# Second attention of an encoder kernel: stationary values for both heads, and inverse sums spread over partitions through memory

## The chip, the cores and the metric

One core of one Trainium2 chip runs the kernel. The metric is the device time of one execution in microseconds (us), given as the median of several runs. The engines are PE (TensorE), DVE (VectorE), ACT (ScalarE), POOL (GpSimd) and SP (SyncE, which only issues transfers). Each works through its own list of instructions in order and is held up only by waits on semaphores. PE adds its products into PSUM, eight banks of 128 x 512 floats.

## What is computed

A trunk of two layers over 512 tokens of 1,024 features. Each layer is a token mixer and then an MLP with squared ReLU and 4,096 hidden features, an RMS norm stands before each, and one more at the end. Layer 0 mixes by neighbourhood attention, layer 1 by the sliding-window attention that the change is about. The reference, cut to that part:

```python
def sliding_window_gqa(h, w_qkv, sinks, rel_table, w_o):   # 16 heads of 64, 4 key/value heads
    ...
    kb, vb = band(k), band(v)                              # 3 key blocks of 128 per query block
    s = jnp.einsum('bnqhgd,bnjhd->bhgnqj', q, kb)          # logits, per block of 128 queries
    s = jnp.where(mask, s + bias, lowest)
    m = jnp.maximum(jnp.max(s, axis=-1, keepdims=True), sink)
    p = jnp.exp(s - m)
    p = p / (jnp.sum(p, axis=-1, keepdims=True) + jnp.exp(sink - m))
    o = jnp.einsum('bhgnqj,bnjhd->bnqhgd', p, vb).reshape(B, S, D)
    return jnp.einsum('bsd,de->bse', o, w_o)
```

## The kernel before

**Data.** Activations lie by feature (128 features on the partitions, 512 tokens along the row). Each float32 operand of a product is split into a high part (what fp32r holds) and a low part, the rest; a product is three matmuls: high x high, high x low, low x high (lines 427 to 429). Weights come as 180 chunks of 512 KB through two buffers: SP loads chunk c (L292) once chunk c-2 has been split, ACT copies out the high part (L839), DVE subtracts for the low part (L1140).

**The second attention.** It works by pairs of heads, 8 pairs, the two heads on key/value heads that lie beside each other in one 128-row tile. A pair has 4 units (n = 0 to 3), one per block of 128 queries, with 2, 3, 3 and 2 key blocks. For a unit:
- PE: scores of both heads (`sw_scores`, L729/L730) into `s_ps`.
- DVE: adds the bias and takes the row's extreme (`sw_logits`, L1232), one instruction per head.
- ACT: exponent and row sum, one per head (`sw_exp`, L918).
- PE: transposes the probabilities, one 128 x 128 block per head and key block (`sw_transpose`, L741), into `pt_ps`.
- ACT copies out the high part (`sw_pt_high`, L923), DVE the low part (`sw_pt_low`, L1189).
- PE: `sw_values` (L752 on, matmuls at L561 and L565): the transposed probabilities are the stationary operand, a head's values the moving one (64 columns of high, 64 of low). Output: 128 tokens on the partitions.

Two units make a group (g = 0, 1). After its second unit DVE (`sw_o_sum`) forms 1/(row sum + sink), adds the two halves of the output (reduce, L1197) and multiplies by the inverse (L1199): tokens lie on partitions, so the inverse is one number per partition. PE transposes that result back to features (`transpose_o`, L574), ACT and DVE split it (`sw_o_high` L1069, `sw_o_low` L1453) for the output projection.

**Order.** It is written out by hand in a `sw_step(m)` for each engine; step m handles pair p = m-1 and interleaves the dense projections of later pairs. PE, for each n: transposes of the unit before, [`transpose_o` at n = 0 and 2], one dense part (3 matmuls of 512 columns), scores of the next unit, a second dense part, values of the unit before. `pt_ps` and `s_ps` hold one unit each. After step 8 the output projection starts: 32 early blocks in the order of `EARLY_BLOCKS`, the last four of which (from the 28th) need the last pair's output.

SP has no order of its own here: it loads chunks in a loop. POOL loads each pair's bias with 8 transfers (L369), two pairs ahead.

```python
for n in range(4):                                  # PE, step m
    if before or n >= 1:
        sw_transpose(*sw_unit_by(p, n, -1))
    ...
    dense_part(2 * n)
    if n < 3 or last != 8:
        sw_scores(*sw_unit_by(p, n, 1))
    dense_part(2 * n + 1)
    if before or n >= 1:
        sw_values(*sw_unit_by(p, n, -1))
```

Of the kernel before, what the change touches and what calls it, by code (L numbers as in the profile page):

```python
# [100 lines left out]
def encoder(nc, xT, wstream, gains, rpb, sinks, rel_table, na_mask, onehot, out):  # L101
    t5_dram = nc.dram_tensor("t5_shifted", (QC, HEADS, T5_W), F32, kind="Internal").ap()
    rpb_dram = nc.dram_tensor("rpb_reversed", (HEADS, RPB_R * PITCH), F32, kind="Internal").ap()

    with ExitStack() as ctx:
# [80 lines left out]
        o_added, o_summed, ot_done, esink_made = sem("o_added"), sem("o_summed"), sem("ot_done"), sem("esink_made")  # L186
# [16 lines left out]
        def f32(ap):  # L203
            return ap.bitcast(F32)
# [67 lines left out]

        def sw_unit_by(p, n, by):

            return p + (n + by) // 4, (n + by) % 4
# [12 lines left out]
        def _(sp):  # L288
# [4 lines left out]

            load_weights(At(0))
# [13 lines left out]
            with sp.Fori((CH_SW + len(SW_FIRST)) // 2, CHUNKS // 2) as i:  # L308
                for n in range(2):
                    load_weights(At(n, 2, i))  # L310
# [113 lines left out]
        def _(pe):  # L424
# [131 lines left out]
            def values(dst, tiles, v_blocks, hh):  # L556

                last = len(tiles) - 1
                for b, (t, n) in enumerate(zip(tiles, v_blocks)):
                    def low():  # L560
                        nc.tensor.matmul(dst[:, HD * hh:HD * (hh + 1)], pt_lo[:, t, :], v_hi[:, n, hh, :], start=False,  # L561
                                         stop=False)
                    if b:
                        low()
                    ins = nc.tensor.matmul(dst, pt_hi[:, t, :], v_parts[:, n, hh, :, :].rearrange("p a b -> p (a b)"),  # L565
                                           start=b == 0, stop=b == last)
                    if not b:
                        low()
                return ins

            def transpose_o(done, bank):
                pe.wait_ge(o_summed, (done + 1).v)
                for jj in range(2):
                    ins = nc.tensor.transpose(bank[:, jj, :], o_tok[:, jj, :, :].rearrange("p a b -> p (a b)"), ident[:])  # L574
                ins.then_inc(ot_done, 1)

# [53 lines left out]
            def output_projection(ch, gr, heads_before, start, bank):  # L630

                early_part(ch, gr, heads_before, start, LAST_OUT)
                if bank is not None:
                    transpose_o(At(heads_before + HEADS - 1), bank)
                else:
# [98 lines left out]
            def sw_transpose(p, n):  # L734
# [3 lines left out]
                at = 0  # L738
                for hh in range(2):
                    for b in range(SW_BLOCKS[n][1]):  # L740
                        ins = nc.tensor.transpose(pt_ps[:, at, :], sw_probs(n, hh)[:, b * P:(b + 1) * P], ident[:])  # L741
                        at += 1
                ins.then_inc(pt_done, 1)

            def sw_values(p, n):

                kb, nb = SW_BLOCKS[n]
                pe.wait_ge(pt_split, (sw_unit(p, n) + 1).v)
                if n % 2 == 0:
                    pe.wait_ge(o_split, (p * 2 + (HEADS - 1 + n // 2)).v)  # L750
                for hh in range(2):
                    ins = values(sw_bank(n // 2)[:, 2 * hh + n % 2, :], range(nb * hh, nb * hh + nb),  # L752
                                 range(4 * p.odd + kb, 4 * p.odd + kb + nb), hh)
                ins.then_inc(pv_done, 1)
# [7 lines left out]
            def sw_step(m, before=True, last=None):  # L762
# [905 lines left out]
```

## Time and profile before

| | |
|---|---|
| device time, median of 3 runs (lowest to highest) | 1143.95 us (1143.48 to 1144.02) |
| time of the profiled execution | 1143.62 us |
| its span in the trace | 1141.9 us |
| TensorE's clock granted over the span | 0.998 of full speed |
| PE, DVE, ACT busy share of the span | 99%, 56%, 45% |
| second attention with its projections | 623.6 to 760 us of the span |
| a step of it (steps 2 to 7) | 15.28 to 15.31 us |

The span is what the trace covers; the 1.7 us between span and time lie around it. Steps were found by the first transposes of a pair's last unit, at 637.63, 652.93, 668.21, 683.49, 698.78, 714.09 and 729.38 us.

### The profile page before, as it was taken

Reading aid. Unit: us, or ns where it says so; the run is one execution under the profiler, and the core shown is the slowest. Engines: PE = TensorE matmul, PEld = TensorE weight load, DVE = VectorE, ACT = ScalarE, POOL = GpSimd, SP = SyncE. Lnnn points to the kernel's source line nnn. Section 1 sums busy time; section 2 is a strip of 40 time slices with the busy share of each in tenths; the row PEclk is TensorE's granted clock in tenths of the full one; section 3 lists DMA queues with packets and bytes.
Section 4 is the critical chain, followed back from the end, with each engine's and each line's share of the span. In section 5 each row is a group of like instructions: output and inputs, shape, how many; then the busy total and the mean of one; then the engine's idle time right before and its main releaser. Section 6 shows DMA issues by size and latency. Waiting matters only on the chain.

```text
span 1141.9 us, 16574 instructions
## 1 busy us (share of the span) xinstructions
PE 1130.5 (99%) x5580; PEld 943.7 (83%) x5580; DVE 638.3 (56%) x1030; ACT 513.1 (45%) x922; POOL 141.5 (12%) x243
## 2 busy tenths in 40 slices
PE   8999999999999999999999999999999999999997
PEld 6888888888888888888888888988888888888886
DVE  7788887764442234544346888866443223444334
ACT  6777677553331124433235676644443122333221
POOL 6544341330000000000001222100000000000000
PEclk9999999999999999999999999999999999999999
DMA  6332221333322332222322122122222222232222
GB/s 227 95 89 92 91 91 55 92 120 102 100 92 92 100 102 92 92 98 86 110 92 92 43 59 62 52 92 93 92 92 98 105 92 92 96 106 92 92 92 93
DMA packets 34290, 106.97 MB, mean 94 GB/s; under 512 B 5760, under 2 KB 8096, under 8 KB 34256
## 3 DMA queue, kind: packets, MB, share of 16 engines
q1 hardware_dynamic: 29344, 98.61, 25.8%
q0 software_dynamic: 4768, 7.90, 3.0%
q8 instruction: 20, 0.33, 0.1%
q14 instruction: 14, 0.11, 0.0%
q10 hardware_dynamic: 144, 0.02, 0.0%
HBM read 103.84 MB, written 2.67 MB: 93 GB/s over the span
## 4 chain that ended last, share of the span: by engine, by line
PE 98%; DVE 1%; ACT 0%; issue 0%; DMA 0%; DVEq 0%; ACTq 0%
PE acc L427 28%; PE acc L428 28%; PE acc L429 28%; PE om_ps L565 2%; PE pt_ps L741 2%; PE om_ps L589 1%; PE om_ps L561 1%; PE s_ps L531 1%; PE pt_ps L552 1%; PE s_ps L730 1%; PE s_ps L729 1%; PE om_ps L521 1%; PE s_ps L427 1%; PE s_ps L428 1%; PE s_ps L429 1%; DVE sqsum L1262 0%
## 5 line engine op out<-in xcount | busy, mean ns | idle before, releaser
L839 ACT CAST w_hi<-w_raw 128x1024 fp32r<-128x1024 f32 x179 | 188.3, 1052 | 391.9 <-PE acc L429 386.9
L427 PE MATMUL acc<-h_hi,w_hi 128*128 128x512 f32 x792 | 315.6, 398 | 1.0 <-DVE h_lo L1252 0.5
L429 PE MATMUL acc<-h_hi,w_lo 128*128 128x512 f32 x792 | 308.8, 390 | 0.0
L428 PE MATMUL acc<-h_lo,w_hi 128*128 128x512 f32 x792 | 308.8, 390 | 0.0
L1140 DVE TENSOR_TENSOR w_lo<-w_raw,w_hi 128x1024 fp32r<-128x1024 f32 x177 | 217.7, 1230 | 141.4 <-ACT w_hi L839 140.8
L427 PE MATMUL acc<-u_hi,w_hi 128*128 128x512 f32 (+1 forms) x624 | 240.7, 386 | 0.0
L429 PE MATMUL acc<-u_hi,w_lo 128*128 128x512 f32 (+1 forms) x624 | 239.5, 384 | 0.0
L428 PE MATMUL acc<-u_lo,w_hi 128*128 128x512 f32 (+1 forms) x624 | 239.4, 384 | 0.0
L427 PEld LDWEIGHTS acc<-h_hi,w_hi 128*128 128x128 f32 x792 | 148.7, 188 | 32.9 <-issue 1.7
L429 PEld LDWEIGHTS acc<-h_hi,w_lo 128*128 128x128 f32 x792 | 148.7, 188 | 31.7
L428 PEld LDWEIGHTS acc<-h_lo,w_hi 128*128 128x128 f32 x792 | 148.9, 188 | 28.4 <-issue 0.7
L1169 DVE SCALAR_TENSOR_TENSOR scaled<-acc,rstd 128x512 f32<-128x512 f32 x90 | 61.9, 689 | 138.8 <-PE acc L429 137.2
L427 PEld LDWEIGHTS acc<-u_hi,w_hi 128*128 128x128 f32 x624 | 117.3, 188 | 23.3 <-DVE w_lo L1140 0.5
L429 PEld LDWEIGHTS acc<-u_hi,w_lo 128*128 128x128 f32 x624 | 117.2, 188 | 23.1
L428 PEld LDWEIGHTS acc<-u_lo,w_hi 128*128 128x128 f32 x624 | 117.3, 188 | 22.5
L1314 DVE TENSOR_TENSOR x_res<-acc,x_res 128x512 f32 (+1 forms) x39 | 26.9, 691 | 99.5 <-PE acc L429 99.5
L918 ACT ACTIVATE probs<-probs,nmax 128x256 f32<-128x256 f32 (+1 forms) x128 | 67.4, 531 | 9.5 <-DVE nmax L1232 9.3
L352 POOL TENSOR_TENSOR bias_masked<-bias_pairs,mask 128x256 f32<-128x256 f32 x64 | 52.6, 859 | 83.3 <-DVE nmax L1232 81.4
L1179 DVE TENSOR_TENSOR u_lo<-scaled,u_hi 128x512 f32 (+1 forms) x72 | 53.6, 744 | 13.1 <-ACT u_hi L893 13.1
L923 ACT CAST pt_parts<-pt_ps 128x1024 fp32r<-128x1024 f32 (+2 forms) x48 | 38.5, 802 | 45.5 <-PE pt_ps L741 38.1
L1189 DVE TENSOR_TENSOR pt_parts<-pt_ps,pt_parts 128x1024 fp32r<-128x1024 f32 (+2 forms) x48 | 46.0, 957 | 14.6 <-ACT pt_parts L923 14.2
L410 POOL CAST u_hi<-u_hi 64x512 fp32r<-64x512 f32 x4 | 3.4, 858 | 365.5 <-DVE u_hi L1479 365.3
(158 smaller groups left out, 1076.3 us busy)
## 6 DMA issues: line engine op xcount, KB each, us to landing
w_raw<-in_wstream SPq DMA_DIRECT2D x180, 512.0 KB, 3.3
bias_pairs<-rpb_reversed POOLq DMA_DIRECT2D x64, 62.0 KB, 2.4
bias_pairs<-t_shifted POOLq DMA_DIRECT2D x64, 48.0 KB, 2.5
x_res<-in_xT SPq DMA_DIRECT2D x8, 256.0 KB, 5.5
out_y<-x_res SPq DMA_DIRECT2D x8, 128.0 KB, 1.8
out_y<-x_res SPq DMA_DIRECT2D x4, 256.0 KB, 2.3
t_shifted<-vT POOLq DMA_DIRECT2D x16, 31.0 KB, 2.1
mask<-in_mask POOLq DMA_DIRECT2D x1, 64.0 KB, 5.3
```

The lines of the kernel that those rows point to most:

```text
L352: ins = nc.gpsimd.tensor_tensor(bias_m[:, g, i, :, :].rearrange("p c r -> p r c"), rows[:, :, U0[j]:U0[j] + WC], mask[:, j:j + 1, :].to_br ...
L427: nc.tensor.matmul(dst, a[0], b[0], start=start, stop=False)
L428: nc.tensor.matmul(dst, a[0], b[1], start=False, stop=False)
L429: return nc.tensor.matmul(dst, a[1], b[0], start=False, stop=stop)
L839: nc.scalar.copy(w_hi[:, c.odd, :], w_raw[:, c.odd, :]).then_inc(w_hi_made, 1)
L918: return nc.scalar.activation(src, src, ACT.Exp, bias=nmax[:, slot, i:i + 1], scale=-1.0, accum_out=rsum[:, slot, i:i + 1])
L923: nc.scalar.copy(pt_hi[:, 0:blocks, :], pt_ps[:, 0:blocks, :]).then_inc(pt_hi_made, 1)
L1140: nc.vector.tensor_tensor(w_lo[:, c.odd, :], w_raw[:, c.odd, :], f32(w_hi[:, c.odd, :]), ALU.subtract).then_inc(w_split, 1)
L1169: nc.vector.scalar_tensor_tensor(out=dst, in0=order(bank), scalar=factor, in1=order(rstd[:]), op0=op, op1=ALU.mult).then_inc(acc_taken, 1)
L1179: nc.vector.tensor_tensor(order[0](dst), order[1](scaled[:, e.odd, :]), order[0](f32(hi)), ALU.subtract).then_inc(tile_split, 1)
L1189: nc.vector.tensor_tensor(pt_lo[:, 0:blocks, :], pt_ps[:, 0:blocks, :], f32(pt_hi[:, 0:blocks, :]), ALU.subtract).then_inc(pt_split, 1)
L1314: nc.vector.tensor_tensor(x[:, k.v, :], acc[g.odd][:], x[:, k.v, :], ALU.add).then_inc(acc_taken, 1)
```

## The change

For the second attention alone:
- **Values.** A stationary operand now is one key block's values of both heads side by side (128 columns: head 0, head 1), high or low. The moving operand is the transposed probabilities of both heads and of one or both units of the group: 256 or 512 columns. A group takes 9 matmuls: two key blocks that both units need (3 each, 512 columns) and one that only one unit needs (3 of 256 columns). Of the output, the rows of a head are used only in that head's columns. It lies by feature, so `transpose_o` and the reduce are dropped.
- **Place.** The values of group 0 run at the end of n = 2, those of group 1 at the end of n = 0 of the next step; none run at n = 1 and n = 3.
- **Inverse sums.** They must now lie along the row, the same on all 64 partitions of a head. SP stores the 128 x 4 inverses transposed to memory (4-byte runs), waits for that, and loads them back twice, each time 1 KB to 64 partitions. These steps (`turn_inverse`) stand in SP's list before and after the loads of weights, which are written out for the 8 steps.
- **Normalisation.** `sw_normalise` multiplies PSUM by the spread inverses, one instruction per head, at the head of DVE's n = 0 (group 0) and after the logits of n = 2 (group 1). The probabilities lie in a free part of `u_lo`, the values' parts in another order, the spread inverses in `vT`.
- **ACT.** `sw_o_high` now reads SBUF; it and `queries_high` stand ahead of the exponents, and the sinks of group 1 behind the split of weights.

The diff, cut to its core:

```diff
@@ SP
+            def turn_inverse(p, g):
+                sp.wait_ge(den_made, (p * 4 + (HEADS + 2 * g + 2)).v)
+                if p.a >= 1:
+                    sp.wait_ge(o_summed, (p * 2 + (HEADS - 1 + g)).v)
+                sp.dma_start(rden_dram[g].rearrange("t q -> q t"), dens_of(rden, g), allow_slow_non_contiguous=True).then_inc(rden_stored, 16)
+                sp.wait_ge(rden_stored, (p * 32 + 16 * (g + 1)).v)
+                for hh in range(2):
+                    sp.dma_start(sw_rden[HEAD_ROWS[hh], g, :], rden_dram[g, 2 * hh:2 * hh + 2, :].rearrange("t q -> (t q)").partition_broadcast(HD)
+                                 ).then_inc(rden_landed, 16)
+            def sw_step(m, before=True):
+                if before:
+                    turn_inverse(m + -2, 1)
+                load_weights(m + (CH_SW + 7))
+                turn_inverse(m + -1, 0)
...
+            for m in range(1, PAIRS + 1):
+                sw_step(At(m), before=m > 1)
+            turn_inverse(At(7), 1)
@@ PE
-            def sw_values(p, n):
...
+            def sw_values(p, g):
+                pe.wait_ge(pt_split, (sw_unit(p, 2 * g + 1) + 1).v)
+                pe.wait_ge(o_summed, (p * 2 + (HEADS - 1 + g)).v)
+                dst = flat(sw_bank(g)).rearrange("p (h u q) -> p h u q", h=2, u=2)
+                def products(b, units, start=False, stop=False):
+                    block = 4 * p.odd + g + b
+                    stationary = [t[:, block, :, :].rearrange("p h d -> p (h d)") for t in (sw_v_hi, sw_v_lo)]
+                    for n, (v, t) in enumerate(((0, 0), (0, 1), (1, 0))):
+                        ins = nc.tensor.matmul(dst[:, :, units, :], stationary[v], sw_pt[:, t, b, :, units, :],
+                                               start=start and n == 0, stop=stop and n == 2)
+                    return ins
+                both, only = ((0, 1), 2) if g == 0 else ((1, 2), 0)
+                products(both[0], slice(0, 2), start=True)
+                products(only, slice(1 - g, 2 - g))
+                products(both[1], slice(0, 2), stop=True).then_inc(pv_done, 2)
@@ PE, sw_step
-                    if n == 0 and before:
-                        transpose_o(p * 2 + (HEADS - 2), sw_bank(0))
-                    if n == 2 and before:
-                        transpose_o(p * 2 + (HEADS - 1), sw_bank(1))
...
-                    if before or n >= 1:
-                        sw_values(*sw_unit_by(p, n, -1))
+                    if n == 0 and before:
+                        sw_values(p + -1, 1)
+                    if n == 2:
+                        sw_values(p, 0)
@@ PE, after step 8
-            early_part(CH_SWO, GR_SWO, HEADS, 12, 14)
-            transpose_o(At(2 * HEADS - 2), sw_bank(0))
-            early_part(CH_SWO, GR_SWO, HEADS, 14, 16)
-            sw_values(At(7), 3)
-            output_projection(CH_SWO, GR_SWO, HEADS, 2 * BLOCKS, sw_bank(1))
+            early_part(CH_SWO, GR_SWO, HEADS, 12, 16)
+            sw_values(At(7), 1)
+            output_projection(CH_SWO, GR_SWO, HEADS, 2 * BLOCKS, False)
@@ ACT, sw_step
                     if before or n >= 1:
                         sw_pt_high(*sw_unit_by(p, n, -1))
+                    if n == 0 and before:
+                        sw_o_high(p + -1, 0)
+                    if n == 2 and dense:
+                        queries_high(m)
                     sw_exp(p, n, 0)
                     sw_exp(p, n, 1)
-                    if n % 2 == 1:
-                        sw_sinks(p, n // 2)
-                    if n == 0 and before:
-                        sw_o_high(p + -1, 0)
+                    if n == 1:
+                        sw_sinks(p, 0)
                     if n == 2 and before:
                         sw_o_high(p + -1, 1)
-                    if n == 2 and dense:
-                        queries_high(m)
                     if n == 3:
                         split_weights(m + (CH_SW + 6))
+                        sw_sinks(p, 1)
@@ DVE
-            def sw_o_sum(p, g):
...
+            def sw_normalise(p, g):
+                dve.wait_ge(pv_done, (sw_unit(p, 2 * g + 1) + 1).v)
+                dve.wait_ge(rden_landed, (p * 64 + 32 * (g + 1)).v)
+                dve.wait_ge(o_split, (p * 2 + (HEADS + g)).v)
+                bank = flat(sw_bank(g)).rearrange("p (h n) -> p h n", h=2)
+                for hh in range(2):
+                    rows = HEAD_ROWS[hh]
+                    ins = nc.vector.tensor_tensor(sw_o[rows, :], bank[rows, hh, :], sw_rden[rows, g, :], ALU.mult)
+                ins.then_inc(o_summed, 1)
@@ DVE, sw_step
                 for n in range(4):
+                    if n == 0 and before:
+                        sw_normalise(p + -1, 0)
                     if before or n >= 1:
                         sw_pt_low(*sw_unit_by(p, n, -1))
-                    if n == 0:
-                        split_weights(m + (CH_SW + 5))
-                    if n == 1 and before:
-                        sw_o_sum(p + -1, 1)
-                    if n == 3:
-                        sw_o_sum(p, 0)
                     if n < 3 or dense:
                         sw_logits(*sw_unit_by(p, n, 1))
+                    if n == 0 and before:
+                        sw_inverse(p + -1, 1)
+                    if n == 0:
+                        split_weights(m + (CH_SW + 5))
                     if n == 0 and before:
                         sw_o_low(p + -1, 0)
                     if n == 1 and dense:
                         scale_queries(m)
+                    if n == 1:
+                        sw_inverse(p, 0)
+                    if n == 2 and before:
+                        sw_normalise(p + -1, 1)
+                    if n == 2 and dense:
+                        queries_low(m)
                     if n == 2 and before:
                         sw_o_low(p + -1, 1)
```

`sw_inverse` is the sum and the reciprocal that stood in `sw_o_sum`.

## Rows read from the trace of the kernel before

**Rows 1.** The page, part 1: busy time and share of the span, by engine.

```profile
PE 1130.5 (99%) x5580; PEld 943.7 (83%) x5580; DVE 638.3 (56%) x1030; ACT 513.1 (45%) x922; POOL 141.5 (12%) x243
```

**Rows 2.** Stretches, steps 3 and 8: length, PE, PEld, DVE, ACT, POOL busy; clock.

```profile
652.93:668.21 15.28, 15.28 (x106) 13.65 (x106) 13.69 (x35) 10.61 (x29) 4.42 (x11) 1.00 0.21 62
729.38:744.68 15.30, 14.80 (x103) 13.24 (x102) 11.65 (x32) 9.37 (x27) 0.00 (x0) 1.00 0.11 35
```

**Rows 3.** Chain of waits, 652.93 to 668.21: shares by line, then pieces (start, us).

```profile
by line: PE om_ps L565 17.7%; PE pt_ps L741 14.9%; PE om_ps L561 12.4%; PE acc L427 12.3%; PE acc L428 12.3%; PE acc L429 12.2%; PE s_ps L730 7.8%; PE s_ps L729 7.7%; PE om_ps L574 2.9%; issue 0.0%
...
660.65 0.22 PE om_ps L574 x2
660.87 0.23 PE acc L427
...
661.69 0.12 PE s_ps L730
...
662.86 0.19 PE om_ps L561 x2
663.06 0.14 PE om_ps L565
...
666.66 0.33 PE om_ps L565
```

**Rows 4.** DVE groups, steps 3 to 7 (652.93 to 729.38), shapes apart: busy, mean ns.

```profile
L1232 DVE CUSTOM_DVE_ANT_0 probs<-s_ps,bias_pairs,sw_nsink 128x384 f32<-128x384 f32 x20 | 11.5, 612 | 0.0
L1189 DVE TENSOR_TENSOR pt_parts<-pt_ps,pt_parts 128x768 fp32r<-128x768 f32 x10 | 9.6, 958 | 3.1 <-ACT pt_parts L923 3.0
L1232 DVE CUSTOM_DVE_ANT_0 probs<-s_ps,bias_pairs,sw_nsink 128x256 f32<-128x256 f32 x21 | 9.3, 481 | 0.1
L1189 DVE TENSOR_TENSOR pt_parts<-pt_ps,pt_parts 128x512 fp32r<-128x512 f32 x10 | 6.9, 692 | 3.8 <-ACT pt_parts L923 3.8
L1197 DVE TENSOR_REDUCE o_raw<-om_ps 128x256 f32<-128x512 f32 x10 | 6.9, 691 | 0.3
...
L1199 DVE TENSOR_TENSOR o_tok<-o_raw,rden 128x256 f32<-128x256 f32 x10 | 4.2, 425 | 0.3
...
L1443 DVE RECIPROCAL rden<-rden 128x4 f32<-128x4 f32 x10 | 1.8, 178 | 0.3
L1440 DVE TENSOR_TENSOR rden<-rsum,esink 128x4 f32<-128x4 f32 x10 | 1.5, 155 | 0.0
```

**Rows 5.** ACT groups of the same stretch.

```profile
L918 ACT ACTIVATE probs<-probs,nmax 128x384 f32<-128x384 f32 x20 | 12.2, 612 | 0.0
L918 ACT ACTIVATE probs<-probs,nmax 128x256 f32<-128x256 f32 x20 | 10.0, 505 | 0.1
L923 ACT CAST pt_parts<-pt_ps 128x768 fp32r<-128x768 f32 x10 | 8.0, 802 | 10.8 <-PE pt_ps L741 10.8
L918 ACT ACTIVATION_READ_ACCUMULATOR probs<-probs,nmax 128x1 f32 x40 | 7.6, 190 | 0.0
L923 ACT CAST pt_parts<-pt_ps 128x512 fp32r<-128x512 f32 x10 | 5.9, 588 | 12.3 <-PE pt_ps L741 12.3
L839 ACT CAST w_hi<-w_raw 128x1024 fp32r<-128x1024 f32 x5 | 5.2, 1033 | 0.0
L1061 ACT ACTIVATE esink<-nmax,sw_sink 128x2 f32<-128x2 f32 x20 | 4.7, 283 | 0.0
```

**Rows 6.** First attention, DVE on 64 partitions, one source in PSUM: min/median/max ns.

```profile
L1220 DVE TENSOR_TENSOR o_tok<-om_ps,o_tok x16: 416/417/418, 46.0 to 213.0; 64x256 f32<-64x256 f32 x16
```

**Rows 7.** Transfers: KB each, median us to landing; then SP's own time to issue one.

```profile
out_y<-x_res SPq DMA_DIRECT2D x8, 128.0 KB, 1.8
out_y<-x_res SPq DMA_DIRECT2D x4, 256.0 KB, 2.3
bias_pairs<-t_shifted POOLq DMA_DIRECT2D x64, 48.0 KB, 2.5
L292 SPq DMA_DIRECT2D w_raw<-in_wstream x180: 328/333/417, 0.9 to 1113.4; - x180
```

**Rows 8.** Weight loads in steps 3 to 7: KB each, median us to landing.

```profile
w_raw<-in_wstream SPq DMA_DIRECT2D x5, 512.0 KB, 4.0
```

More of the change, by code:

```diff
@@ L271, in half_blocks, with dens_of, sw_pt_part @@
             return t[:, 256 * hh:256 * (hh + 1)]
+        sw_v = v_parts[:].rearrange("p n h t d -> p n (h t d)").rearrange("p n (t h d) -> p n t h d", t=2, h=2)
+        sw_v_hi, sw_v_lo = sw_v[:, :, 0, :, :], sw_v[:, :, 1, :, :]
+        sw_pt = u_lo[:, 10:16, :].rearrange("p a b -> p (a b)").rearrange("p (t b h u q) -> p t b h u q", t=2, b=3, h=2, u=2)
+        sw_rden = vT[:].rearrange("p (g n) -> p g n", g=2)
+        sw_o = o_tok[:].rearrange("p h j d -> p (h j d)")
+        def dens_of(t, g):
+            return t[:, g, :, :, :].rearrange("p a b c -> p (a b c)")
+        def sw_pt_part(t, n):
+            first, blocks = SW_BLOCKS[n]
+            first -= n // 2
+            return sw_pt[:, t, first:first + blocks, :, n % 2, :].rearrange("p b h q -> p (b h) q")
         def sw_unit_by(p, n, by):
@@ L307, in _ @@
                 load_weights(At(CH_SW + n), CH_SW + place)
-            with sp.Fori((CH_SW + len(SW_FIRST)) // 2, CHUNKS // 2) as i:
+            for n in range(6, 8):
+                load_weights(At(CH_SW + n))
+            for m in range(1, PAIRS + 1):
+                sw_step(At(m), before=m > 1)
+            turn_inverse(At(7), 1)
+            with sp.Fori((CH_SWO + 4) // 2, CHUNKS // 2) as i:
                 for n in range(2):
@@ L554, in na_transpose @@
                 ins.then_inc(pt_done, 1)
[L556 to L575, printed above, removed]
             def outputs_read(units):
@@ L737, in sw_transpose @@
                 pe.wait_ge(pt_split, unit.v)
[L738 to L742, printed above, removed]
-                ins.then_inc(pt_done, 1)
-            def sw_values(p, n):
[L747 to L754, printed above, removed]
+                for b in range(SW_BLOCKS[n][1]):
+                    for hh in range(2):
+                        ins = nc.tensor.transpose(pt_ps[:, 2 * b + hh, :], sw_probs(n, hh)[:, b * P:(b + 1) * P], ident[:])
+                ins.then_inc(pt_done, 1)
+            def sw_values(p, g):
[13 more added lines that the diff above has]
+                products(both[1], slice(0, 2), stop=True).then_inc(pv_done, 2)
             def sw_v_blocks(kv):
@@ L1448, in sw_pt_low, with sw_inverse @@
-            def sw_pt_low(p, n):
-                pt_low(sw_unit(p, n), 2 * SW_BLOCKS[n][1])
+            def sw_inverse(p, g):
+                made = p * 4 + (HEADS + 2 * g)
+                dve.wait_ge(esink_made, (p * 2 + (g + 1)).v)
+                nc.vector.tensor_tensor(dens_of(rden, g), rsum[:, g, :], esink[:, g, :], ALU.add).then_inc(den_made, 1)
+                dve.wait_ge(den_made, (made + 1).v)
+                nc.vector.reciprocal(dens_of(rden, g), dens_of(rden, g)).then_inc(den_made, 1)
@@ new lines, in sw_pt_low @@
+            def sw_pt_low(p, n):
+                dve.wait_ge(pt_hi_made, (sw_unit(p, n) + 1).v)
+                nc.vector.tensor_tensor(sw_pt_part(1, n), pt_ps[:, 0:2 * SW_BLOCKS[n][1], :], f32(sw_pt_part(0, n)),
+                                        ALU.subtract).then_inc(pt_split, 1)
+            def sw_normalise(p, g):
[3 more added lines that the diff above has]
+                bank = flat(sw_bank(g)).rearrange("p (h n) -> p h n", h=2)
+                for hh in range(2):
+                    rows = HEAD_ROWS[hh]
+                    ins = nc.vector.tensor_tensor(sw_o[rows, :], bank[rows, hh, :], sw_rden[rows, g, :], ALU.mult)
+                ins.then_inc(o_summed, 1)
@@ L1499, in sw_step @@
                         scale_queries(m)
+                    if n == 1:
[4 more added lines that the diff above has]
+                        queries_low(m)
                     if n == 2 and before:
                         sw_o_low(p + -1, 1)
-                    if n == 2 and dense:
-                        queries_low(m)
                     if n == 3 and not dense:
```

70 lines of the change are left out of this document (27 added, 43 removed).

## The prediction

> **What bounds the kernel now.** I read the busy shares first: PE is busy for 1130.5 of 1141.9 us [rows 1], so only what PE does or waits for can move the time. Next the stretches of the second attention: a step takes 15.28 us, PE is busy throughout, at the full clock (2.4 GHz), DVE for 13.69 and ACT for 10.61 [rows 2]. DVE has 1.6 us of slack a step, less than it seems if PE gets faster. Last the chain of waits in a step [rows 3]: all of it is PE. Its pieces give PE's real pace, which the 0.22 to 0.48 us of a single matmul hide: 0.23 for 512 columns, 0.12 for 256, 0.11 for one transpose, and 0.14 and 0.10 for the values' matmuls of 128 and 64 columns. One piece is 0.33 where 0.14 is the pace: PE waited 0.19 there for the low parts of the probabilities.
>
> **PE work.** Old values: (17.7 + 12.4)% of 15.28 = 4.60 us a step with that wait, 4.40 without. Transposes of the output: 2.9% = 0.44 [rows 3]. New values: per pair 12 matmuls of 512 columns and 6 of 256: 12 x 0.23 + 6 x 0.12 = 3.5 us. Columns streamed double (3,840 to 7,680), but 40 matmuls become 18, and the old ones go at a pace that hardly falls with their columns (0.14 for 128, 0.10 for 64). PE per step: 15.28 - 4.60 - 0.44 + 3.5 = 13.74; net of the wait a pair saves 1.34, eight pairs 10.7.
>
> The pieces show a 64-column matmul at 0.10 and a 128-column one at 0.14. The Trainium skill, TensorE: Matmul & The Clock Gate, section Back-to-back issue gap, gives an isolated warm gap of N/2.4 + 2.5 ns, some 25 ns for 64 columns and 56 for 128, and by it the change would be a loss: 40 old matmuls 1.6 us and four transposes 0.2 against 12 x 0.216 + 6 x 0.109 = 3.2, some 11 us slower over 8 pairs. By that rule the trace does not go: 40 old matmuls take 4.40 us.
>
> **New waits of PE.** With no values at n = 1 and 3, PE comes round to the next transposes sooner. Between transposes and what follows it has two dense parts, 6 x 0.23 = 1.40, and scores, 4 x 0.12 = 0.47 or, at 0.175 each (7.8% + 7.7% less those 0.95), 0.70: 1.87 or 2.10 us. What it then waits for:
> - Transposes at n = 0 need unit 3's exponents: ACT copies 0.80, two exponents 2 x 0.51 and the readout 0.19 [rows 5], 2.0; 0.1 less for overlap, and 0.25 to restart PE (the 0.19 above and a hand-off): 2.15 against 1.87, a wait of 0.3.
> - At n = 2: 0.59 + 2 x 0.61 + 0.19, likewise 2.15, against 2.10: 0.05.
> - Values at n = 2: copy 0.80, subtract 0.96 [rows 4, 5], restart 0.25: 2.0 against 1.87, 0.15 (the present wait, kept).
> - Values at n = 0: ACT first does the weight split 1.03 and, moved behind it, the sinks 2 x 0.28, then copy 0.59; DVE subtracts 0.69: 3.1 with the restart, against 0.25 + 0.46 + 2.10 = 2.8. Wait 0.3.
> Together 0.8; part of each delay is shared by the next, so I take 0.7: a step of 14.45.
>
> **DVE and ACT.** Per group a reduce (0.69) and a product (0.43) go [rows 4], two products on 64 partitions come; the nearest row is 0.42 [rows 6]. DVE per step: 13.69 - 2 x 1.12 + 4 x 0.42 = 13.1 of 14.45 us. The subtraction for the low part stays. DVE becomes 91% busy, but its logits and subtractions still come just in time; if its order fitted badly, it could add some 0.3 a step. ACT only changes its source and order (10.6 us). POOL's bias transfers begin up to 1.5 us later with the sinks; they are issued in 4.4 us and land in 2.5 [rows 2, 7], needed over 11 us on: nothing. Chunk loads are issued some 4 us later behind a waiting SP, but have a step in hand: nothing. If that cover were gone, each step would carry it.
>
> **The transfers.** The trace shows no store in 4-byte runs. The store of 128 KB (128 runs of 1 KB) lands in 1.8 us, that of 256 KB (256 such runs) in 2.3 [rows 7]: 4 ns a run. The new store has 512 runs: 2.3 + 256 x 0.004 = 3.3 us. Lower end 1.8 (tiny runs free), upper 5.3 (a run at twice the price). I take 3.3, the extrapolation. A load back of 64 runs lies between 1.8 and the bias's 2.5: 2.2. Issuing costs SP 0.35 each [rows 7].
>
> SP does both groups' transfers in turn, and waits for each store, s. That makes a loop: from a step's first normalisation to the inverse of group 1, DVE takes 2 x 0.42, subtraction 0.69, logits 2 x 0.61 and 0.15 + 0.18 [rows 4, 6], less overlaps: 2.85. Then s and 0.8 for hand-off and two loads' issue, the chunk's issue 0.35, the second store s, and 2.65 until its later load lands, on which the next step's first normalisation waits: 2s + 6.65. The second store is issued just behind a chunk of 512 KB on the same queue, which lands in 4.0 [rows 8]; I add up to 1.4 for that. At 3.3 the loop is 13.3 to 14.7 us: beside PE's 14.45, on the edge. So I take 14.5 a step. The skill's page DMA: Bandwidth & Descriptors, section Anatomy of one DMA, fits a transfer by 2.0 us plus bytes/436 KB per us, for those POOL issues; by that s is 2.0, the loop at most 12.1, and the step 14.45. No row here has this form.
>
> **Ends.** In step 1, step 8 (DVE only 11.65 [rows 2]) and the output projection the other 10.7 - 6 x 1.34 = 2.7 us come off PE, with perhaps 0.5 of waits: 2.2. The last pair's path (copy, subtract, inverse, store, load, normalise, split) takes about 0.6 + 0.7 + 0.3 + 3.3 + 3.1 + 0.8 + 0.8 = 9.6 us from its last transposes. Before block 28 PE has 16 blocks of 3 x 0.23 and the group's values, 1.75, together 12.8: it fits up to s = 6.5.
>
> **Sum.** Six steps x (15.29 - 14.5) = 4.7, ends 2.2: 6.9 off. Against the profiled execution (span 1141.9, time 1143.62) 1136.7; the median of the runs lies 0.3 above it: 1137.0.
>
> **The rivals.**
> - Transfers set the pace (slower). With s = 4.5 and 1.4 for the chunk the loop is 17.05: six steps lose 10.6, ends give 2.2: 1152. It decides from a step of 15.66 on, s = 3.8 (4.5 if the chunk costs nothing). For it: SP serves both groups in turn, runs of 4 bytes, bias transfers at the same time. Against: 3.3 from two rows. 0.29. It would show as DVE idle before the normalisation, and PE before the values.
> - The loop a little too long: s 3.5 to 4, a step of 15.0 to 15.7, time 1140 to 1144. 0.14.
> - The hand-offs cost nothing: steps of 13.74, 9.3 + 2.7 off, 1132. Against it: the wait that is there already, and ACT's copy and exponents. 0.07.
> - PE's cost goes by columns alone, 0.23 per 512 (slower): the old values would be 3,840 columns, 1.7 us, the transposes 0.2, the new 3.5, so 1.6 a pair lost and 1157. The rows have the old ones at 4.40, so 0.01. The rule of the clock page above is of this kind.
>
> **How the numbers follow.** Forecast case 0.49: 1134 to 1139. A measurement can tell about 0.2%, 2.3 us, from no change. Faster by more: 0.49 + 0.07 + not quite half of the second rival, 0.06 = 0.62; within that 0.10; slower 0.28 (the first rival, less what is so near the edge that it can't be told, and the last). The range leaves out the steps above s = 4.3 and a twentieth below: 1132.5 to 1150. The forecast's own is 1134 to 1139.
>
> **What would show it.** Steps of 14.3 to 14.7; values' matmuls at 0.23 and 0.12 on the chain; no output transposes; PE waits of 0.2 to 0.3 before transposes at n = 0 and values; DVE near 13.1 a step; the store landing in 2.4 to 3.4. Wrong if DVE idles for the loads (transfers), if steps are under 14 (hand-offs hidden), or if the new matmuls go slower than 0.23.

## The result, and the profile after

The changed kernel takes 1255.76 us (median of 6 runs, 1253.79 to 1256.41), the kernel before, run beside it, 1143.79. The ratio is 1.0975, interval 1.0964 to 1.0986: 112 us slower, where 7 us faster was forecast, and far outside the range of 1132.5 to 1150. The profiled execution has a span of 1252.1 us.

The page of the changed kernel (busy rows; granted clock in 40 slices; chain; groups of part 5; DMA issues):

```profile
PE 1152.0 (92%) x5372; PEld 949.7 (76%) x5372; DVE 634.4 (51%) x1030; ACT 513.9 (41%) x922; POOL 140.9 (11%) x243
...
PEclk9999999999999999999987787778999999999999
...
PE 78%; DMA 15%; DVE 3%; issue 2%; SPq 2%; ACT 0%; DVEq 0%; ACTq 0%
...
L467 PE MATMUL acc<-u_hi,w_hi 128*128 128x512 f32 (+1 forms) x624 | 242.5, 389 | 7.9 <-DVE u_lo L1468 7.9
...
L770 PE MATMUL om_ps<-u_lo,v_parts 128*128 128x512 f32 (+1 forms) x144 | 42.9, 457 | 45.9 <-DVE u_lo L1453 45.4
...
L1463 DVE TENSOR_TENSOR o_tok<-om_ps,vT 64x256 f32<-64x256 f32 x32 | 13.5, 422 | 107.8 <-DMA vT<-inverse_sums 95.4
...
bias_pairs<-t_shifted POOLq DMA_DIRECT2D x64, 48.0 KB, 3.6
...
vT<-inverse_sums SPq DMA_DIRECT2D x32, 64.0 KB, 3.8
```

PE was the bound for 99% of the span [rows 1]; now for 22% of it something else is on the chain, and that is DMA with DVE's and SP's hand-offs behind it. DVE's products are short (422 ns, as the 417 of [rows 6]), but DVE idles 107.8 us before them, 95.4 of them for the loads of the inverses: close to the 112 us lost. The slices with a clock of 7 and 8 are the second attention.

The same kernel, two steps of it, and two stretches of 1 us; columns as in [rows 2]:

```profile
677.00:706.50 29.50, 19.65 (x79) 15.94 (x79) 13.23 (x35) 10.80 (x29) 4.35 (x10) 0.73 0.25 41
706.50:736.10 29.60, 17.25 (x79) 13.87 (x79) 13.26 (x36) 10.80 (x29) 4.34 (x10) 0.85 0.19 40
706.50:707.50 1.00, 1.00 (x5) 0.90 (x5) 1.00 (x2) 0.00 (x0) 0.00 (x0) 0.50 0.03 0
708.50:709.50 1.00, 1.00 (x8) 0.84 (x7) 0.00 (x0) 0.30 (x1) 0.00 (x0) 1.00 0.00 0
```

A step takes 29.5 us in place of 15.28, with DVE and ACT doing what was forecast (13.2, 10.8). Now the chain through the second of these steps (start, length, what), which answers to [rows 3]:

```profile
706.54 8.53 DMA inverse_sums<-rden
...
715.09 0.45 SPq L319
...
715.58 0.60 SPq L319
...
716.22 0.58 SPq L309
...
716.90 13.13 DMA inverse_sums<-rden
...
730.04 0.45 SPq L319
...
730.54 2.62 DMA vT<-inverse_sums
...
733.61 0.43 DVE o_tok L1463
...
735.94 0.19 DVE rden L1449
...
736.15 11.19 DMA inverse_sums<-rden
```

Not one piece is PE. Group 1's store, two loads, the chunk, group 0's store, its loads, the normalisation, the logits, the inverse, and again the store: the loop that the prediction wrote down as the way to lose. Nor does PE stand on the chain anywhere from 655 to 848 us. The store's own times, minimum, median and maximum of 16, are in the answer on `rden`, the tile that it reads:

```profile
DMA to landing us min/median/max: 8.3/10.1/13.1
```

It is not bandwidth. The DMA view of 706 to 709 us, in 40 slices of 0.075 us, shows when the 528 packets of the store at 706.54 keep the DMA engines busy:

```profile
DMA  0000000000000000000487840000000000000000
...
DMA packets 528, 0.00 MB, mean 1 GB/s; under 512 B 528, under 2 KB 528, under 8 KB 528
```

From 707.42 to 707.80, and nothing after; the same view up to 716 us shows no other packet. The store is told as done at 715.07: for the last 7.3 of its 8.5 us the DMA engines are idle.

### The profile page after: what moved, and what is told of

The parts are those of the page before. It is cut to its first block, busy times and chain, and to the rows that moved or that the text cites. A ratio compares the mean times of both kernels' runs of the same rounds, so it can differ in the third digit from the quotient of the medians.

```text
span 1252.1 us, 16200 instructions
## 1 busy us (share of the span) xinstructions
PE 1152.0 (92%) x5372; PEld 949.7 (76%) x5372; DVE 634.4 (51%) x1030; ACT 513.9 (41%) x922; POOL 140.9 (11%) x243
## 4 chain that ended last, share of the span: by engine, by line
PE 78%; DMA 15%; DVE 3%; issue 2%; SPq 2%; ACT 0%; DVEq 0%; ACTq 0%
PE acc L467 24%; PE acc L468 24%; PE acc L469 24%; DMA inverse_sums<-rden 13%; DMA vT<-inverse_sums 2%; PE s_ps L571 1%; PE om_ps L608 1%; PE pt_ps L592 1%; SPq L319 1%; DVE probs L1241 1%; PE om_ps L561 1%; SPq L309 0%; DVE sqsum L1271 0%; DVE o_tok L1463 0%; PE s_ps L467 0%
## 5 line engine op out<-in xcount | busy, mean ns | idle before, releaser
L467 PE MATMUL acc<-h_hi,w_hi 128*128 128x512 f32 x792 | 318.8, 402 | 1.6 <-DVE h_lo L1261 1.2
L467 PE MATMUL acc<-u_hi,w_hi 128*128 128x512 f32 (+1 forms) x624 | 242.5, 389 | 7.9 <-DVE u_lo L1468 7.9
L467 PEld LDWEIGHTS acc<-h_hi,w_hi 128*128 128x128 f32 x792 | 150.9, 191 | 33.6 <-issue 2.3
L468 PEld LDWEIGHTS acc<-h_lo,w_hi 128*128 128x128 f32 x792 | 150.7, 190 | 28.3 <-issue 0.7
L467 PEld LDWEIGHTS acc<-u_hi,w_hi 128*128 128x128 f32 x624 | 118.2, 189 | 31.7 <-DVE u_lo L1468 8.3
L770 PE MATMUL om_ps<-u_lo,v_parts 128*128 128x512 f32 (+1 forms) x144 | 42.9, 457 | 45.9 <-DVE u_lo L1453 45.4
L770 PEld LDWEIGHTS om_ps<-u_lo,v_parts 128*128 128x128 f32 x144 | 29.9, 248 | 56.7 <-DVE o_tok L1463 28.8
L1463 DVE TENSOR_TENSOR o_tok<-om_ps,vT 64x256 f32<-64x256 f32 x32 | 13.5, 422 | 107.8 <-DMA vT<-inverse_sums 95.4
L1201 DVE TENSOR_TENSOR u_lo<-scaled,u_hi 128x512 f32 (+1 forms) x72 | 53.6, 744 | 13.1 <-ACT u_hi L912 13.1
```

Source lines behind the costliest of these rows:

```text
L467: nc.tensor.matmul(dst, a[0], b[0], start=start, stop=False)
L468: nc.tensor.matmul(dst, a[0], b[1], start=False, stop=False)
L770: ins = nc.tensor.matmul(dst[:, :, units, :], stationary[v], sw_pt[:, t, b, :, units, :], start=start and n == 0, stop=stop and n == 2)
L1201: nc.vector.tensor_tensor(order[0](dst), order[1](scaled[:, e.odd, :]), order[0](f32(hi)), ALU.subtract).then_inc(tile_split, 1)
L1463: ins = nc.vector.tensor_tensor(sw_o[rows, :], bank[rows, hh, :], sw_rden[rows, g, :], ALU.mult)
```

## The experiments

In the first, in those that load `xT`, and in the one with a single group, some or all of the products multiply by something other than the inverse sums, so that part of the softmax's division is left out; in the one with runs of 16 bytes the inverses go to other tokens. The times of a store are read from SP's own timeline, as the time from its issue to the issue of the first load, which waits for it. The runs with a store of another form in which the loads read `xT` were executed once each, so the smallest differences between their kernel times (1136 and 1138 us, say) carry nothing; each has 16 stores, and the argument goes by these.

**No transfers.** DVE fills the spread inverses with 1 once; SP only loads weights.

```diff
-                sw_step(At(m), before=m > 1)
-            turn_inverse(At(7), 1)
+                load_weights(At(m + CH_SW + 7))
```

> The changed kernel without its transfers: the spread inverses are a constant 1, written once by DVE, and SP only loads weights, so the division by the sums is left out. Theory (the transfers alone cost the 112 us): the predicted step of 14.3 to 14.6 us comes back, 1135 to 1139 us in all, PE at full clock. Rival A (the new order of PE, ACT and DVE is itself slow): steps over 15.3 and 1145 us or more. Rival B (hand-offs cost nothing): steps of 13.7 to 13.9, 1132 us.

Measured: 1136.04 us, ratio 0.9933 (0.9917 to 0.995). Two of its steps:

```profile
655.43:669.76 14.33, 14.17 (x81) 11.57 (x79) 13.01 (x35) 10.70 (x29) 4.41 (x11) 1.00 0.24 66
669.76:684.08 14.32, 14.13 (x80) 11.56 (x79) 13.01 (x35) 10.70 (x29) 4.11 (x10) 1.00 0.23 64
```

Everything in the change but the transfers gains 7.7 us. The whole loss, 120 us, is the transfers. The new values' matmuls, nine a group, on its chain:

```profile
660.59 2.02 PE om_ps L769 x9
...
667.99 1.77 PE om_ps L769 x9
```

Together 3.8 us, where 3.5 and waits of up to 0.45 were forecast: that fits the pace of 0.23 and 0.12 us which the prediction took.

**Runs of 16 bytes.** The same 2 KB, each partition's four values together.

```diff
-                sp.dma_start(rden_dram[g].rearrange("t q -> q t"), dens_of(rden, g), ...)
+                sp.dma_start(rden_dram[g].rearrange("t q -> (t q)").rearrange("(q t) -> q t", t=QT), dens_of(rden, g))
```

> The changed kernel with the store as it lies: 128 runs of 16 bytes in place of 512 runs of 4 (2 KB either way); the order of the inverses in memory is then another, so tokens are divided by other tokens' sums. The loads back are the same 64 x 1 KB. Theory (the store's 10 us go by its runs, about 8 us for 512): about 2 + 2 = 4 us, step near PE's 14.5 to 16, total 1137 to 1150. Rival C (a round trip through memory costs its 10 us whatever the runs): store 8 to 10, total above 1230.

Measured: 1137.75, ratio 0.9948 (0.9928 to 0.9968); store 2.6 us. SP waits for each store and takes the groups in turn here too, so these alone are not the loss; the form of this store is.

**512 runs, 64 bytes apart**, and then **16** and **8** bytes apart. The count and size of the runs stay, only the gaps between them differ (a last dimension of 16, 4 or 2 floats, of which the first is written).

```diff
-    rden_dram = nc.dram_tensor("inverse_sums", (2, QT, P), F32, kind="Internal").ap()
+    rden_dram = nc.dram_tensor("inverse_sums", (2, QT, P, 16), F32, kind="Internal").ap()
...
-                sp.dma_start(rden_dram[g].rearrange("t q -> q t"), ...
+                sp.dma_start(rden_dram[g, :, :, 0].rearrange("t q -> q t"), ...
```

> 512 runs of 4 bytes as in the changed kernel, but 64 bytes apart in memory; the loads back read 64 x 1 KB of an input instead (so no division by the sums). If neighbouring 4-byte writes hold each other up, the store falls from 10.1 to about 3 to 4 us and the total to about 1140. If each run has its price wherever it goes, the store stays at 8 to 11 us and the total above 1220.

> All 512 runs of 4 bytes, 16 bytes apart, so four to a line of 64 bytes; the loads back read an input (so no division by the sums). Theory L: like the store in 16-byte runs, four to a line, 2.6 us, or up to 3.5 with 512 runs; total 1136 to 1140. Rival (a 4-byte write always costs, and 64 bytes apart was only far enough for some wider unit): 5 us or more, total over 1150.

> 512 runs of 4 bytes, 8 bytes apart, so 64 to a stretch of 512 bytes, between the changed kernel (128 to a stretch, 8.3 us at the least) and e6_four (32, 2.6 at the least); the loads back read an input (so no division by the sums). Theory (the price goes by how many writes fall close together): 4 to 5.5 us, total 1155 to 1185. Rival (only writes that touch each other are dear): 2.6 to 3.5 us, total 1143.

Measured: 64 bytes apart 1136.39 us, store 2.4; 16 apart 1143.41, store 3.5; 8 apart 1156.61, store 4.4; touching 10.1. At 64 bytes the 512 runs take 0.6 us more than 128 do (1.8, the next pair). The number of runs costs little. Their nearness does.

**A quarter of the runs**, touching, and the same 64 bytes apart.

```diff
-                sp.dma_start(rden_dram[g].rearrange("t q -> q t"), dens_of(rden, g), ...
+                sp.dma_start(rden_dram[g, 0:1, :].rearrange("t q -> q t"), dens_of(rden, g)[:, 0:1], ...
```

> A quarter of the store: 128 runs of 4 bytes, neighbours, one row of the four; the loads back read an input instead (so no division by the sums). If the price goes by runs: about 2 + 2 = 4 us, as with 128 runs of 16 bytes. If it goes by bytes or is fixed: 2 us or 10 us.

> 128 runs of 4 bytes, 64 bytes apart; the loads back read an input (so no division by the sums). Against e4_quarter (the same 128 runs as neighbours, 7.3 us) it changes the distance alone. Theory: 1.4 to 1.9 us, total 1136. If the number of runs or their 4 bytes were the price: 7 us, total 1200.

Measured: touching 1203.61, store 7.3; apart 1138.01, store 1.8 (minimum, median and maximum of 16, touching and apart):

```profile
DMA to landing us min/median/max: 6.1/7.3/8.9
...
DMA to landing us min/median/max: 1.4/1.8/4.2
```

A fourth of the writes saves only a fourth of the time as long as they touch.

**Which nearness?** 128 writes again, in other places and other orders. The destination's dimensions, strides in floats:

```diff
+ e5_lines          [[256, 8], [1, 16]]    8 places 1 KB apart, 16 touching in each, from neighbouring partitions
+ e13_shared_lines  [[1, 4], [256, 32]]    32 places 1 KB apart, 4 touching in each, from partitions 32 apart
+ e14_own_lines     [[16, 4], [256, 32]]   the same order, nothing touching
+ e16_own_near      [[32, 8], [1, 16]]     as the first, places 128 bytes apart
+ e17_shared_far    [[1, 16], [256, 8]]    as the first, from partitions 8 apart
```

> 128 runs of 4 bytes as in e4_quarter (whose store took 7.3 us), but laid as 8 groups of 16 neighbours, 1 KB from group to group; the loads back read an input (so no division by the sums). Theory L (writes into the same 64 bytes of memory take turns at some 0.4 us each): 16 to a line as before, so the store stays at 6 to 8 us, total about 1200. Rival M (turns are taken within a larger stretch, 512 bytes or more): 16 in place of 128 in the stretch, so the store falls to 2 to 2.6 us, total about 1137.

> The store writes 128 values (one in four of a group) to 32 places 1 KB apart, in each of them 4 neighbouring values that 4 different DMA engines write; the loads read other memory of the same form, so the sums are left out. Density theory (many writes fall into a short stretch of memory, whoever writes them): each 64 bytes take four writes, as few as where 16-byte gaps were left and the store took 3.5 us; store 1.6 to 2.6 us, time 1136.5 to 1141. Sharing theory (several DMA engines write into the same 64 bytes and take turns there): one engine's 16 neighbouring writes a line took 3.05 us, four engines in one line should take what the touching 128 writes took, 5 to 8 us; time 1170 to 1205.

> The same 128 values and the same queue order, but the four neighbours lie 64 bytes apart, so that each line of 64 bytes is written once. Both theories: store 1.4 to 2.2 us, time 1136 to 1140. If it is as long as the run with the shared lines, the form of the access (its order over partitions) sets the time and neither theory is told apart.

> The run with 8 lines of 16 touching writes, 1 KB apart (store 3.05 us), with its lines moved to 128 bytes apart: each line has its own DMA engine as there, and 128 writes fall into 1 KB as with the 8-byte gaps (512 writes, 4.4 us). The two runs before this one left the sharing of a line with 4 writes in it harmless (2.5 against 2.3 us), so two readings are left. Stretch theory (what counts is how many writes fall within about a KB): as dense as the 8-byte gaps in number of writes, near the quarter store that took 7.3: store 4 to 7 us, time 1150 to 1190. Line theory (dear are many writes into one line by several engines): each line has one engine, store 2.5 to 3.6 us, time 1139 to 1144.

> 8 lines of 16 touching writes, 1 KB apart, with the access turned so that each of the 16 neighbours in a line comes from another group of partitions, and so from another DMA engine. Stretch theory: as the run with 8 lines of one engine each, store 2.5 to 3.6 us, time 1138 to 1143. Line theory: full lines written by many engines, as the quarter store, 5 to 8 us, time 1165 to 1205.

Measured, with all the stores of this study in one table (from SP's timelines):

| runs | where | writes within 1 KB | within 256 B | store, median (min) us | kernel us |
|---|---|---|---|---|---|
| 512 x 4 B | touching (the change) | 256 | 64 | 10.1 (8.3) | 1255.76 |
| 128 x 4 B | touching, 512 B in all | 128 | 64 | 7.3 (6.1) | 1203.61 |
| 512 x 4 B | 8 B apart | 128 | 32 | 4.4 (3.1) | 1156.61 |
| 128 x 4 B | 8 places of 16, 128 B apart | 128 | 32 | 4.2 (2.7) | 1151.01 |
| 512 x 4 B | 16 B apart | 64 | 16 | 3.5 (2.6) | 1143.41 |
| 128 x 4 B | 8 places of 16, 1 KB apart | 16 | 16 | 3.0 (1.9) | 1141.02 |
| same, other partitions | same | 16 | 16 | 3.1 (1.8) | 1138.74 |
| 128 x 4 B | 32 places of 4, 1 KB apart | 4 | 4 | 2.5 (2.0) | 1136.22 |
| 512 x 4 B | 64 B apart | 16 | 4 | 2.4 (1.8) | 1136.39 |
| 128 x 4 B | same order as the 32 places, none touching | 4 | 4 | 2.3 (2.0) | 1135.63 |
| 128 x 4 B | 64 B apart | 16 | 4 | 1.8 (1.4) | 1138.01 |

The theory that the writes to one piece of 64 bytes take turns there fell with the 8 places: as full as in the quarter store, yet 3.0 against 7.3. The theory that it is dear when those writes come from several DMA engines fell too, above all with the run that takes 16 neighbours from partitions 8 apart (3.1 us; the one from partitions 32 apart, 2.5, has only 4 neighbours in a place). The trace does not name the DMA engine of a packet, so that these come from different engines is assumed from the partitions.

These five stores differ from the quarter store in one more thing. In the first store of each run the quarter store shows 144 packets, 16 more than it has runs; the 8 places show 136, at either distance, the 32 places 132. If the surplus counts the DMA engines in use, which no run here shows, they used 8 and 4 in place of 16. That isn't what makes 3.0 of 7.3: the run with the other partitions shows 144 again and takes 3.1. Nor does it touch the comparison of the two distances, one store near the median of each:

```profile
660.62 0.64 SPq L316 DMA_DIRECT2D inverse_sums<-rden  x1
663.67 2.89 SPq L319 DMA_DIRECT2D vT<-in_xT  x2
...
712.44 0.64 SPq L317 DMA_DIRECT2D inverse_sums<-rden  x1
716.64 1.14 SPq L320 DMA_DIRECT2D vT<-in_xT  x2
```

Moving the 8 places from 1 KB to 128 bytes apart, with nothing else changed, takes the store from 3.0 to 4.2 us and the kernel from 1141.0 to 1151.0, at the lower edge of what the stretch theory expected.

So density counts, but over which stretch? Counted within 1 KB it does not order the table: 128 writes take 7.3, 4.4 and 4.2 us, and 16 take 3.1 and 1.8. Counted within 256 bytes it does: 64 writes take 10.1 and 7.3 us, 32 take 4.4 and 4.2, 16 take 3.5, 3.0 and 3.1, 4 take 1.8 to 2.5. Counts within 512 bytes give nearly the same order; those within 64 or 128 bytes miss the two distances, where they are equal. This was read from the layouts when all runs were done, and no run varied that stretch alone.

**One group.** Only group 1 has the slow transfers; group 0's half is filled with 1.

```diff
-                turn_inverse(m + -1, 0)
```

> The changed kernel with the slow stores of group 1 alone; group 0's spread inverses are a constant 1 (its division left out), so SP never has two stores to take in turn. Theory (a step is the loop through both stores on SP): with one store the loop is s + DVE's 7 us + issue and load, 4 to 5: at s = 8.5 to 9, 20 to 21 us a step, total 1172 to 1182. Rival D (one store on DVE's path is enough for the whole loss): above 1235. Third: if group 0's wait was the only one that counted, below 1150.

Measured: 1195.73, ratio 1.0454 (1.0435 to 1.0473). Group 1's stores are issued at 663.12, 684.88 and 705.67, steps of 21.8 and 20.8 us. The chain of such a step:

```profile
640.29 8.51 DMA inverse_sums<-rden
648.82 0.52 SPq L319
649.38 3.71 DMA vT<-inverse_sums
...
655.52 0.58 PE s_ps L745
...
656.73 0.43 PE acc L466
657.16 0.43 PE acc L467
657.59 0.43 PE acc L468
658.01 0.85 PE pt_ps L756 x4
...
663.12 9.64 DMA inverse_sums<-rden
```

So a second cost shows, which the loop of two stores hides: PE, back from its wait, does 512 columns in 0.43 us, not 0.23 [rows 3], and four transposes in 0.85, not 0.44. That is the 1.2 GHz level, seen as a granted clock of 0.50 from 706.5 to 707.5 in the changed kernel after PE had idled, and here it lies on the chain. All seven of its steps average 21.7 us, where 20 to 21 were expected; from the pieces at either pace, the 1.2 GHz level is estimated to cost some 2.5 us of the step shown. The total is 14 us above the range. The longer steps make about 5 of it; the rest lies outside them and was not taken further.

**Two queues.** Group 1's transfers go to POOL's queue.

```diff
@@ POOL, behind the bias transfers of each pair
+                turn_inverse(pair + -2, 1)
```

> The changed kernel, slow stores and all, but group 1's transfers are issued by POOL (in its list behind a pair's bias loads), group 0's by SP, so that the two groups no longer take turns on one queue. Theory (step = 2 stores in turn + about 9): with one store of 10 on the path at a time the step falls from some 29 to 19 to 23 us, total 1165 to 1190. Rival D (the turns don't matter, DVE's waits in order do): within 10 us of the changed kernel's 1256.

Measured: 1230.77, ratio 1.0757 (1.0737 to 1.0777): 25 us faster than the changed kernel, and outside both ranges. Its stores on SP's queue are issued at 654.20, 681.32, 708.69 and 736.33: steps of 27.1 to 27.6 us, later ones 22.8 to 24.6. SP's stores now take 8.0 to 14.3 us, POOL's 9.5 (median). POOL's loads land in 5.2 us where SP's take 3.3. A round on POOL, with DVE's normalisation of group 1 and its next inverse:

```profile
698.98 4.13 POOL L404 DMA_DIRECT2D bias_pairs<-t_shifted  x8 [10.94 <-ACT esink L1086]
...
704.09 0.80 POOL L416 DMA_DIRECT2D inverse_sums<-rden  x1 [0.66 <-DVE rden L1455]
713.74 1.07 POOL L419 DMA_DIRECT2D vT<-inverse_sums  x2 [8.86 <-DMA inverse_sums<-rden]
...
721.92 0.86 DVE L1469 TENSOR_TENSOR o_tok<-om_ps,vT 64x256 f32<-64x256 f32 x2 [11.54 <-issue]
...
731.24 0.18 DVE L1455 RECIPROCAL rden<-rden 128x4 f32<-128x4 f32 x1
```

The dependence from store to store through DVE and PE is there whatever the queue: 9.65 us for the store, 8.2 until the normalisation, 9.3 from there to the next inverse, part of that with PE at 0.43 us for 512 columns. A second queue only takes away the turn-taking. POOL's bias transfers were not in the way of the store at 704.09, for which POOL waited 0.66 us; the next inverse, made at 731.42, was stored only at 732.88. Why the loads on POOL took longer, no run here separates.

**Three versions with the whole computation.** By token: the store in 128 runs of 16 bytes, one load of the whole 2 KB to all partitions, and DVE picks every fourth float. Compact: the same, but POOL copies the floats together first. Rows: PE transposes the 128 x 4 inverses to 4 rows, ACT copies these out, the store is 4 runs of 512 bytes, and all after it is as in the change.

```diff
@@ by token, DVE
+                    inverse = sw_rden[g][rows, :].rearrange("p (q t) -> p t q", t=QT)[:, 2 * hh:2 * hh + 2, :]
@@ rows: PE, ACT, SP
+                nc.tensor.transpose(sw_bank(0)[0:QT, g, :], dens_of(rden, g), ident[:]).then_inc(row_turned, 1)
+                nc.scalar.copy(rden_row[:, g, :], sw_bank(0)[0:QT, g, :]).then_inc(row_made, 1)
+                sp.dma_start(rden_dram[g], rden_row[:, g, :]).then_inc(rden_stored, 16)
```

> A version that is to beat both: the store goes out as it lies (128 runs of 16 bytes, by token), one load brings all four inverses of a token, 2 KB, to every partition, and the normalisation reads every fourth float; group 1 has a buffer of its own. Theory: store 2.6 us, load 2.5 to 3.5, steps of 14.3 to 14.6, 1137 to 1139 us. Rival: reading every fourth float makes the product slower (over 0.6 us in place of 0.42), DVE becomes the bound: 1142 or more.

> e7_by_token with the reading of every fourth float taken off DVE: POOL copies the two wanted inverses of each token side by side (two copies per group), DVE's products read whole rows again. Theory (e7's 4.4 us over e2_runs16 are its products of 0.60 in place of 0.42 us, four a step): products back at 0.42, 1138 to 1140. Rival (the larger load, 256 KB, is what costs, or POOL's copies come late behind its bias transfers): 1141 or more.

> The whole computation. PE turns the 128 x 4 inverses into 4 rows of 128 (one small transpose a group), ACT copies them to SBUF, SP stores 4 runs of 512 bytes and loads them to the partitions as the change does. Theory (only the 4-byte neighbouring writes are dear): store 1.4 to 2.3 us, steps of 14.4 to 14.8, time 1137 to 1141, faster than the kernel before by 0.3 to 0.6%. Rival (the way over PE and ACT costs as much as it saves: ACT's copy stands late behind its other work, PE waits for the inverse before it goes on): steps of 15.0 to 15.6, time 1141 to 1148.

Measured: by token 1142.15, ratio 0.9984 (0.9975 to 0.9993); compact 1147.53, 1.0032 (1.002 to 1.0044); rows 1140.14, **0.9969 (0.9957 to 0.9981)**. In the first two it is the rival's figure that came true. The strided product of the first takes 605 ns in place of 422, 0.73 us of DVE a step. In the second POOL sits idle for over 3.4 us before each pair of copies, so its bias transfers don't delay them; the two copies (0.64 us each) lengthen the way from load to product, and DVE waits for them 11 times between 640 and 750 us, 11.4 us together. The rows version is faster than both kernels, than the one before by 0.3%:

```profile
656.34:671.34 15.00, 14.54 (x83) 11.72 (x82) 13.34 (x35) 11.16 (x32) 4.54 (x11) 1.00 0.32 83
671.34:686.01 14.67, 14.21 (x81) 11.46 (x80) 12.95 (x35) 11.11 (x31) 4.07 (x10) 1.00 0.28 78
```

```profile
L787 PE MATMUL om_ps<-ident,rden x16: 269/271/273, 630.6 to 743.6; 128*4 128x128 f32 x16
```

```profile
L1109 ACT COPY rden_row<-om_ps x16: 255/256/257, 630.9 to 743.9; 4x128 f32<-4x128 f32 x16
```

Its stores take 1.7 us (median), and two small instructions a group make the path that the 4-byte runs replaced. It keeps 3.6 of the 7.7 us that the first experiment showed to be there; its steps are 0.35 to 0.7 us longer than 14.32. The stretch from its first to its last store is 113.0 us (631.19 to 744.22), in the changed kernel 217.5 (630.54 to 848.04): 104.5 of the 113.6 us between their spans. Nearly all of the other 9 follow the last store (9.8, less 0.65 before the first).

## Why the prediction was wrong

- **The step that failed is the store's size.** "4 ns a run" came from stores whose runs are 1 KB long [rows 7], and was carried on to runs of 4 bytes that touch: 3.3 us taken, 5.3 as the upper end. Measured 8.3 to 13.1, median 10.1. The count was the wrong variable: 512 runs 64 bytes apart take 2.4 us. The upper end was a choice (double the price of a run) and not a bound, since no row had short or touching runs. And the range did not even reach it: 1150 is a store of 4.3 us, while 5.3 gives a loop of 18.65 and some 1162. So it was too narrow by construction.
- **The loop was right.** 2s + 6.65 with the measured s of 8.53 and 13.13 gives 28.3 us; the step is 29.6. The missing 1.3 are small terms: hand-off and the loads' issue 1.15 for 0.8, the chunk's issue 0.68 for 0.35, the later load 3.13 for 2.65, DVE 2.99 for 2.85. Stores behind a chunk (group 0's, from the second on) average 11.0 us, group 1's 9.4: the term for the chunk, up to 1.4, was 1.7. The rival "Transfers set the pace" named place, form and sign, and had 0.29; it priced s at 4.5 and the total at 1152. One mis-sized term of a loop that was written down in full turned the direction.
- **The loads.** 2.2 forecast, 3.8 measured in the changed kernel (median of 32), 2.6 in the rows version.
- **PE, DVE and ACT were right**, as the run without transfers shows: steps of 14.32 (forecast 14.45), DVE 13.0 (13.1), ACT 10.7 (10.6), total 1136.04 (1137.0). The waits for the exponents before the transposes were there, as waits of PE's weight loads: 3.0 us in 9 waits over five steps, none longer than 0.5.
- **The ends.** "It fits up to s = 6.5" held as a condition, and was broken: the last store took 10.21 and its load 5.17, and PE idled 7.9 us in the output projection for the last low part (the row of L467 above). The sum let the loop cost six steps and had the ends gain 2.2 us. Beside the rows version, six steps (647.32 to 824.82 against 641.89 to 730.39) lose 89.0 of the 113.6 us; the other 25 are ends: 6.1 between the first two stores, 9.4 before the last, 9.8 behind it.
- **Covers at nothing.** No instruction waited for a chunk from 655 to 850 us, though they landed in 3.9 to 13.6; POOL's bias landed in 3.6 in place of 2.5, and no logits waited for it. Both stayed free.
- **A lower clock** was not in the prediction. Two steps of the changed kernel show 0.73 and 0.85 granted and 19.65 and 17.25 us of busy PE for what takes 14.1 at the full clock. In its loop no PE work is on the chain, so this cost nothing there. Behind the wait of 7.9 us in the output projection the first matmuls on the chain take 0.43 us each, and with one slow group they stand in every step.
- **The Trainium skill's rules.** The Trainium skill, DMA: Bandwidth & Descriptors, Anatomy of one DMA, puts a fixed 2.0 us plus bytes by rate on a transfer issued by POOL, and most of those 2 us down to the receipt from the memory written. The stores here are SP's. For separated runs the traces are near it (1.8 to 2.4 us for 0.5 and 2 KB); for touching ones they are not, by a factor of five. That the DMA engines are busy for 0.4 us and the end is told 7 us later agrees with a time that passes at the memory. The same page's Specifications say that below 512 bytes a transfer does a read-modify-write. Every 4-byte run here is below that, the cheap ones too, so it alone doesn't set the price; whether such writes to one stretch follow each other is a reading that fits the table, and no run here shows it.

## What to carry to other kernels

Before a layout is turned round by a DMA, look at where the short writes land, not only at how many there are: a store of 512 4-byte writes that touch in memory took 10 us here, and a small transpose on PE (0.27 us) with a copy (0.26 us) brought it to 1.7. A step in a loop that ends in a store, a wait and a load has to be priced with a true upper end; where the trace has no transfer of that form, the range must reach to where the loop's formula goes if the price is several times the guess. And a loop of transfers is set by the longest way round it, so a second queue takes away only the turn-taking: here 25 of 112 us.

## What was not expected of the hardware

- Stores of 512 runs of 4 bytes land in 10.1 us when the runs touch, 4.4 with 8 bytes from one to the next, 3.5 with 16, 2.4 with 64; stores of 128 such runs in 7.3 (touching) and 1.8 (64).
- The DMA engines are idle for most of that: in the store at 706.54 the packets end 1.3 us after the issue, the completion comes 7.3 us later.
- The order of the writes over the partitions did not matter (3.0 against 3.1 us), the distance of their groups did (3.0 against 4.2).
- PE came back from a wait at the 1.2 GHz level: idle 6.4 us until 705.28, granted 0.50 from 706.5 to 707.5 and 1.00 from 708.5 to 709.5.
- The issue of a 64-partition load took SP 0.45 and 0.60 us, that of a chunk 0.58 behind it, against 0.33 before [rows 7]. The stores of the five runs with places took 0.56 to 0.63 to issue, the other 4-byte ones 0.33 to 0.37.

What stays open: over how many bytes nearness counts, which the table puts near 256 to 512 without a test of its own, and by which mechanism. Touching writes in places 1 KB apart cost 1.2 us more than single ones 64 bytes apart, of which 0.3 is SP's own time to issue the store.
